# Two transformer blocks on one core: waits moved at the first key unit, at the hand-overs between stages, in the recurrence and at the end

## The reference

```python
# block 1
hx = modulate(rms_norm(x, g_pre_mix), sh_m, sc_m)      # sh_m, sc_m ... from silu(c) @ w_mod + b_mod
hc = modulate(rms_norm(ctx, g_pre_mix), csh_m, csc_m)
...                                                     # attention and retention of hx @ w_in, hc @ w_in
x_new = x + gt_m * rms_norm(mix_x, g_post_mix)
x_new = x_new + gt_f * rms_norm(swiglu(hf, w_ffn_in, w_ffn_out), g_post_ffn)
# block 2
x = x + 0.5 * swiglu_2(rms_norm_2(x, ffn1_norm), ffn1_gate, ffn1_up, ffn1_down)
z = rms_norm_2(x, mix_norm) @ w_in                      # zq, zf, zi, zg, zb, zc, zu
o_h = hgrn2_chunkwise(q, 1 - f, zi, log(f))             # the recurrence, f from zf and lb_param
y_conv = zb * causal_depthwise_conv(zc * zu, conv_w)
x = x + concat(y_hgrn, y_conv) @ w_out
km, vm = split(rms_norm_2(mem, mem_norm) @ w_kv_mem)    # memory attention
x = x + att @ w_o_mem
x = x + 0.5 * swiglu_2(rms_norm_2(x, ffn2_norm), ffn2_gate, ffn2_up, ffn2_down)
return rms_norm_2(x, final_norm)
```

## Time and profile before

| | |
|---|---|
| median of 3 runs | 1061.64 us (1059.79 to 1061.7) |
| the profiled execution's own time | 1061.17 us |
| its span in the trace | 1059.4 us |
| TensorE busy | 1020.1 us, 96% of the span |
| VectorE busy | 596.0 us, 56% |
| ScalarE busy | 494.4 us, 47% |
| mean DMA rate over the span | 178 GB/s |
| weight units transferred | 156 of 1024 KB |

### The profile page before, as it was taken

One profiled execution on the slowest core, in us unless ns is written; L12 is line 12 of the kernel. 1 busy time (PEld: TensorE's weight loads), 2 busy tenths in 40 slices (PEclk: granted clock), 3 DMA queues, 4 the chain that ended last, 5 costly groups with the idle time before them and its releaser, 6 DMA issues.

```text
span 1059.4 us, 13255 instructions
## 1 busy us (share of the span) xinstructions
PE 1020.1 (96%) x5148; PEld 834.7 (79%) x5148; DVE 596.0 (56%) x689; ACT 494.4 (47%) x598; POOL 0.2 (0%) x4
## 2 busy tenths in 40 slices
PE   4989999999999999999999999999999999999996
PEld 3867876897788888888888887788878778888885
DVE  4186386766755554475555545857666456555543
ACT  6253446646543444364444433674346445444431
POOL 0000000000000000000000000000000000000000
PEclk8999999999999999999999999999999999999998
DMA  9928585003554555556555555443243236455541
GB/s 370 417 88 321 208 299 217 28 1 120 199 188 170 198 187 174 194 181 212 183 187 184 184 198 191 163 178 136 80 159 130 109 119 217 181 189 186 179 159 40
DMA packets 26542, 188.71 MB, mean 178 GB/s; under 512 B 2944, under 2 KB 3200, under 8 KB 3968
## 3 DMA queue, kind: packets, MB, share of 16 engines
q1 hardware_dynamic: 25920, 185.63, 48.2%
q10 hardware_dynamic: 576, 2.43, 0.6%
HBM read 187.00 MB, written 1.05 MB: 178 GB/s over the span
## 4 chain that ended last, share of the span: by engine, by line
PE 90%; DVE 5%; ACT 2%; issue 1%; DMA 1%; SPq 0%; DVEq 0%; ACTq 0%
PE bank L1739 25%; PE bank L1741 25%; PE bank L1740 25%; PE bank L1814 2%; DVE w_lo L1129 2%; PE bank L2118 1%; PE bank L1795 1%; PE bank L2011 1%; PE bank L2000 1%; DMA raw<-in_weights 1%; PE bank L2211 1%; ACT w_hi L626 1%; PE bank L2322 1%; PE bank L2048 1%; PE bank L2027 1%
## 5 line engine op out<-in xcount | busy, mean ns | idle before, releaser
L1129 DVE TENSOR_TENSOR w_lo<-raw,w_hi 128x2048 fp32r<-128x2048 f32 (+1 forms) x149 | 338.6, 2276 | 272.5 <-ACT w_hi L626 272.4
L626 ACT ACTIVATE w_hi<-raw 128x2048 fp32r<-128x2048 f32 x148 | 283.1, 1916 | 261.2 <-PE bank L1741 249.4
L1739 PE MATMUL bank<-w_hi,hT_hi 128*128 128x512 f32 (+1 forms) x848 | 335.2, 395 | 7.5 <-issue 5.0
L1741 PE MATMUL bank<-w_hi,hT_lo 128*128 128x512 f32 (+1 forms) x848 | 329.7, 389 | 0.0
L1740 PE MATMUL bank<-w_lo,hT_hi 128*128 128x512 f32 (+1 forms) x848 | 329.3, 388 | 0.0
L1739 PEld LDWEIGHTS bank<-w_hi,hT_hi 128*128 128x128 f32 x848 | 159.7, 188 | 47.2 <-issue 10.9
L1741 PEld LDWEIGHTS bank<-w_hi,hT_lo 128*128 128x128 f32 x848 | 159.6, 188 | 33.6
L1740 PEld LDWEIGHTS bank<-w_lo,hT_hi 128*128 128x128 f32 x848 | 159.8, 188 | 31.3 <-issue 0.2
L1739 PE MATMUL bank<-w_hi,gT_hi 128*128 128x512 f32 x264 | 103.3, 391 | 0.0
L1741 PE MATMUL bank<-w_hi,gT_lo 128*128 128x512 f32 x264 | 102.8, 389 | 0.0
L1740 PE MATMUL bank<-w_lo,gT_hi 128*128 128x512 f32 x264 | 102.7, 389 | 0.0
(11 more groups left out here) (286 smaller groups left out, 993.2 us busy)
## 6 DMA issues: line engine op xcount, KB each, us to landing
raw<-in_weights SPq DMA_DIRECT2D x156, 1024.0 KB, 4.8
arena<-in_first_mods SPq DMA_DIRECT2D x8, 1024.0 KB, 18.0
memV<-in_own_mods SPq DMA_DIRECT2D x8, 1024.0 KB, 4.8
arena<-in_const ACTq DMA_DIRECT2D x1, 1088.0 KB, 5.0
memV<-in_mem SPq DMA_DIRECT2D x1, 1024.0 KB, 6.8
x_res<-in_x SPq DMA_DIRECT2D x1, 1024.0 KB, 18.0
arena<-in_ctx SPq DMA_DIRECT2D x1, 1024.0 KB, 13.8
out<-xn SPq DMA_DIRECT2D x2, 512.0 KB, 2.7
```

The source lines that it names most:

```text
L626: act.activation(w_hi[:, v_slot, :], raw[:, u_slot, :], ACT.Copy).then_inc(hi_ready, 1)
L1129: ins = dve.tensor_tensor(w_lo[:, v_slot, n], raw[:, u_slot, n], w_hi[:, v_slot, n].bitcast(F32), ALU.subtract)
L1739: pe.matmul(out, hi, rhi, start=start, stop=False)
L1741: return pe.matmul(out, lo, rhi, start=False, stop=stop)
```

## The change

**The first key unit.** TensorE transposes the memory first and then does modulation unit 0, where it did that unit first. The first key unit goes through a new function, `first_keys`: 16 matmuls of high x high that wait only for ScalarE's parts, 16 of low input x high weight, 16 of high input x low weight. ScalarE and VectorE take two quarters of `memT` ahead of the first weight split and two behind it; ScalarE loads the table of the square root ahead of the memory's arrival. The second keys follow modulation unit 1, and units 2 and 3, 4 and 5, 6 and 7 are done in pairs. Both engines split `W_IN` ahead of the modulation's columns, and six key products stand behind `mod_T(0)` instead of two. The banks of the keys change:

```diff
-    for u, b in enumerate([0, 1, 3, 0]):
+    for u, b in enumerate([5, 1, 0, 3]):
         plan.streamed(("memK", u), b)
...
```

On ScalarE:

```diff
+            load_table(ACT.Sqrt)
             norm_stats(mem_in, lambda e: e.wait_ge(sem("mem_loaded"), 16))
             norm_scale(mem_in, mem_in)
+            split_T("memT", col("mem_norm"), hi=memT_hi, qs=[0, 1])
             split_to(W_K + 1)
-            split_T("memT", col("mem_norm"), hi=memT_hi)
+            split_T("memT", col("mem_norm"), hi=memT_hi, qs=[2, 3])
...
+            split_to(W_IN + 1)
             mod_row_out(0)
-            split_to(W_IN + 1)
+            split_to(W_IN + 2)
+            split_T(None, shifted=True, hi=hT_hi, qs=[0, 1])
             keys_out(3)
-            split_T(None, shifted=True, hi=hT_hi, qs=[0, 1])
-            split_to(W_IN + 2)
```

On VectorE (the last pieces: `W_IN` split ahead of `mod_columns`, and unit `W_UP[0]` of the first feed-forward split behind its input's parts instead of ahead of them):

```diff
+            split_T("memT", col("mem_norm"), hi=memT_hi, lo=memT_lo, qs=[0, 1])
             low_to(W_K + 1)
-            split_T("memT", col("mem_norm"), hi=memT_hi, lo=memT_lo)
+            split_T("memT", col("mem_norm"), hi=memT_hi, lo=memT_lo, qs=[2, 3])
...
-            low_to(W_K + 4)
+            low_to(W_IN + 1)
             mod_columns(0)
...
-                if n < 3:
+                if 0 < n < 3:
                     low_to(W_IN + n + 1)
...
-            low_to(W_UP[0] + 1)
             split_T("ffn0T", shift=(a_ffn, mod[:, 24:32, 0]))
             low_to(W_UP[0] + 3)
```

```diff
+            def low_last(stage, v, half, outs, first, last, after_high=None, after_input_low=None):
+
+                pe.wait_ge(hi_ready, v + 1)
+                s = v % RING
+                quarters = (2 * half, 2 * half + 1)
+                weights = lambda w, q, e: w[:, s, (2 * (q % 2) + e) * 512:(2 * (q % 2) + e) * 512 + 512]
+                for q in quarters:
+                    pe.wait_ge(sem("T_hi"), T_HI[stage, q])
+                    for e in range(2):
+                        for tb, out in enumerate(outs):
+                            pe.matmul(out[:, :], hT_hi[:, 2 * q + e, tb * P:(tb + 1) * P], weights(w_hi, q, e),
+                                      start=(first and q == quarters[0] and e == 0), stop=False)
+                if after_high:
+                    after_high()
+                for q in quarters:
+                    read_out(pe, (stage, q))
...
+                if after_input_low:
+                    after_input_low()
+                pe.wait_ge(split_ready, v + 1)
...
-            mod_unit(0)
             pe.wait_ge(sem("fixed_loaded"), 16)
             transpose_input("memT", mem_in)
+            mod_unit(0)
+            first_keys()
             mod_unit(1)
-            for q in range(4):
-                read_out(pe, ("memT", q))
-            take(key_products(0), 16)
-            mod_unit(2)
             take(key_products(1), 16)
+            for m in range(2, 4):
+                mod_unit(m)
...
             keys = key_products(3)
             take(keys, 8)
-            mod_unit(6)
-            take(keys, 4)
-            mod_unit(7)
+            for m in range(6, 8):
+                mod_unit(m)
             take(keys, 2)
             mod_T(0)
-            take(keys, 2)
+            take(keys, 6)
...
-                        order.sort(key=lambda o: o[2])
+                        order.sort(key=lambda o: (o[0], o[2]) if f == 2 else o[2])
...
-            transpose_x("ffn2T", added(("mem_out",)))
-            ffn(2, "ffn2T")
+            transpose_x("ffn2T", added(("mem_out",)), [0])
+            ffn(2, "ffn2T", lambda: transpose_x("ffn2T", added(("mem_out",)), [1]))
```

**Ahead of the second mixture.** ScalarE issues two of its three small transfers a stage earlier and the third behind its copies of the input instead of ahead of them:

```diff
-            used(W_DN[1] + UP - 1)
-            for dst, src, name in [(const2, io["const2"], "const2_loaded"),
+            for dst, src, name in [(rows[:, 0, :], io["final_norm"].to_broadcast([P, D]), "final_loaded"),
                                    (lb_p.rearrange("p a n -> p (a n)"), io["lb_param"].to_broadcast([P, D]), "lb_loaded"),
                                    (head_row, io["hgrn_out_norm"].to_broadcast([P, 512]), "head_row_loaded")]:
                 act.dma_start(dst, src).then_inc(sem(name), 16)
-            pre_norm("mix2T", x_added(("down", 1), 0), col("mix_norm"), W_IN2)
+            ffn(1)
+            split_to(W_IN2 + 2)
+
+            split_T("mix2T", col("mix_norm"))
+            used(W_DN[1] + UP - 1)
+            act.dma_start(const2, io["const2"]).then_inc(sem("const2_loaded"), 16)
+            norm_stats(x, x_added(("down", 1), 0))
+            split_to(W_IN2 + 3)
```

The lower bounds of the recurrence's gate (`lb`), with a reciprocal of 512 columns, move on VectorE from behind `pre_norm("mix2T")` into `ffn(1)`, one group behind each of three weight splits; the exponential on ScalarE moves with them:

```diff
+                if f == 1:
+                    dve.wait_ge(sem("lb_loaded"), 16)
+                    chain(dve.tensor_tensor(lb, lb_p[:, 0, :], lb_p[:, 1, :], ALU.max))
+                    dve.tensor_tensor(lb_p[:], lb_p[:], over_heads(lb, 2, 512), ALU.subtract).then_inc(sem("lb_diff"), 1)
+                    low_to(dn + 5)
+                    dve.wait_ge(sem("lb_exp"), 1)
+                    chain(dve.tensor_tensor(lb, lb_p[:, 0, :], lb_p[:, 1, :], ALU.add))
+                    low_to(dn + 6)
+                    chain(dve.reciprocal(lb, lb))
+                    low_to(dn + 7)
...
```

**The recurrence.** The transposes `uT` move into the unit of step 5 (banks 0 and 1), the transposes `bT` ahead of the pair scores of step 6. On ScalarE the copies of `uT` move ahead of `zb`, and the copy `crossT` and the load of the Silu table move behind the two copies of the convolution. On VectorE:

```diff
-            for level in range(LEVELS + 1):
+            for level in range(LEVELS):
...
-                if level == LEVELS:
-                    convolution()
+                if level == LEVELS - 1:
+                    decayed(LEVELS)
                 if level:
                     keep_pairs(level - 1, ("pairs", level - 1))
-                if level == LEVELS:
-                    gated_convolution()
-                else:
-                    low_to(W_IN2 + 9 + level)
+                low_to(W_IN2 + 9 + level)
+                if level == LEVELS - 2:
+                    convolution()
...
+            gated_convolution()
+            keep_pairs(LEVELS - 1, ("pairs", LEVELS - 1))
```

**The end.** The last weight unit of `ffn(2)` is ordered by token block. VectorE and ScalarE then add, square and scale by token block and column half; the second token block's first half is scaled on ScalarE, and `out` leaves in three transfers (512, 256 and 256 KB) instead of two of 512 KB:

```diff
+            dve.wait_ge(sem("last_products"), 1)
+            last_add(0, 0)
+            last_add(0, 1)
+            last_mean(0)
+            dve.wait_ge(sem("last_products"), 2)
+            last_add(1, 0)
+            last_rstd(0)
+            last_out(0, 0)
+            dve.wait_ge(split_used, W_DN[2] + UP)
+            last_add(1, 1)
+            last_mean(1)
+            read_out(dve, ("down", 2, 1, 0))
+            dve.tensor_tensor(xn[:, 1, 0:512], x[:, 1, 0:512], rows[:, 0, 0:512], ALU.mult).then_inc(sem("last_gained"), 1)
+            last_out(0, 1)
+            last_rstd(1)
+            last_out(1, 1)
```

199 lines of the change are left out of this document (134 added, 65 removed).

## The result

The changed kernel took 1049.32 us (median of 4 runs, 1048.3 to 1049.62) against 1061.67 for the kernel before (4 runs, 1059.79 to 1061.72): a ratio of 0.9892, 95% interval 0.9878 to 0.9906. The forecast was 1048.3. The profiled execution took 1049.6 us with a span of 1047.8, which is 11.6 less than before.

The account below looks back on a forecast made before the run. TensorE, busy 96% of the span, was taken as the bound, leaving 39.3 us of idle time and low-clock stretches. Terms summed to 13.1 us off 1061.17, giving 1048.1, taken as 1048.3; range 1042 to 1054.

Parts of the forecast that it names:

- Start: From the kernel's beginning to `W_IN`: key waits, low clock and a context wait go, 8.2 us faster, bounds 6 to 9.
- Chain (c): Start: `W_IN` lands at 43.4 and is split by 47.5, so its first product comes at 49.95, 7.4 us earlier.
- (a): Start: TensorE's own work, which would reach the end of the six key products at 49.
- First feed-forward: First feed-forward: the stall moves to a 1.7 us wait for `w_lo`, 0.4 us slower; bounds -1.7 and +2.7.
- rival (2): Both feed-forwards: the clock falls at the new waits, each fall costing 2.3 us, total 1053 to 1054; chance 0.14.
- Second mixture: Second mixture: earlier hand-over gives -2.3 us, lower bounds moved out -0.9; 3.2 us faster, bounds -2 and -3.8.
- The cover in `ffn(1)`: In `ffn(1)`: 6.8 us free on VectorE hide the moved lower bounds' longest piece, 3.35; failure would cost 1 to 3.
- Memory attention and last feed-forward: Their hand-overs: later half 1 transposes delay low parts and weight splits by 1.65 us, costing +0.5 and +1.6.
- (1): Three hand-overs: `w_lo` is never late and the old waits go too, 21.2 us faster, 1040; chance 0.10.
- (3): Start: transfers bound it, with `W_IN` 5 us later; the gain there would be 3, total 1053.5; chance 0.06.
- (4): Start: slower, the clock stays at 1.2 GHz through the keys, some 22 us more, total 1069; chance 0.03.
- (5): Whole kernel: nothing gained, since the waits are filled by others of the same size all along; chance 0.02.

Follow-up runs that it names:

- e8: Changed kernel, but the first key unit goes through the old function, which waits for all low parts: 1053.29 us.
- e9: Changed kernel, but `W_IN` is split behind the modulation's row and columns again, as before: 1052.28 us.
- e2: Changed kernel, but at `mix2T`, `xattT` and `ffn2T` VectorE splits the second unit between the low parts of quarters 1 and 2: 1044.24 us.
- e4: Changed kernel, but at `xattT` and `ffn2T` all transposes stand ahead of the first unit, as before the change: 1045.81 us.
- e11: Changed kernel with the end as before (last unit's order, adds, norm of whole rows, two scalings, two transfers): 1051.65 us.
- e5: Changed kernel, but the square root's table is loaded ahead of the last feed-forward's norm, with the scratch buffer `warm` left as it was: 1047.77 us.
- e7: Changed kernel with the start (key units, modulation, `W_IN`'s split, table load, banks) put back as before on all three engines: 1057.58 us.
- e10: Changed kernel, but the lower bounds are computed in the second mixture again, behind its norm, instead of in `ffn(1)`: 1053.15 us.
- e3: Changed kernel, but the square root's table is loaded ahead of the last feed-forward's norm, with scratch buffer `warm` one float wider: 1053.09 us.

## Why the prediction was right, and which steps were off

The forecast was 1 us below the measured median, and its sum was off by 1.5 (13.1 for 11.6). By its own words the sum gives 1048.1 + 0.5 = 1048.6 for the median; the 1048.3 has no working. All seven terms have the right sign. The total is closer than its parts, by luck: the start gained 0.9 more than forecast, and the rest 2.4 less. No run takes out the recurrence's edits or the new hand-over at `mix2T`, so these two rest on the distances alone. By its steps:

**Start, -8.2, measured -9.1.** `W_IN` came at 49.95, the very number of the forecast, but for another reason. Chain (c), `W_IN` landing and being split, was said to end last, 1 us behind (a). In the trace the split ends at 47.2 (44.88 and 2.29) and the row waits 0.32 more, until 47.50, for TensorE's own `mod_T`: (a) ended last. e8 shows it (4.6 us on TensorE go straight through) and e9 too (the row stays where it is without the split). The two sums happened to agree, which was luck. The missing 0.8 lay behind `W_IN`: the kernel before has two waits at the context, 0.80 at 64.06 and 0.17 at 65.33, and 1.6 us went with them. The forecast counted the first alone, and at its bracket; a wait costs more than that (last section).

**First feed-forward, +0.4, measured +1.9: the term that was mis-sized.** The stall came where forecast, for `w_lo`, 1.97 for 1.7. Most of the rest was the clock, rival (2), which I had at 0.14. The distance from this wait to the mixture's first product is 382.1 us in the changed kernel (265.34 to 647.45), e2, e4, e9 and e11, and 380.9 to 381.0 in e5, e7, e8 and e10, with the same code in between. Those of 382.1 have a granted clock of 0.5 to 0.6 behind the wait and the others 1.00, all with the same bracket of 1.97 or 1.98. So the fall costs 1.2 us, not the 2.3 that I gave it, and comes in some executions and not in others. A clock of 0.57 over 4 us takes 1.7; some of that is given back, because the slower TensorE comes too late for the next wait. That wait is in every trace without the fall, as in e5, and in none with it:

```profile
267.39 0.47 PE L1804 MATMUL bank<-w_hi,hT_hi 128*128 128x512 f32 x1 [0.18 <-DVE w_lo L1160]
```

Without the fall the term is +0.7: waits of 1.97 and 0.18 for one of 1.72, and 0.25 for the second one's start (last section).

**Second mixture, -3.2, measured -2.7.** Both parts are there: 1.6 us are gained up to the third unit (2.3 forecast; the second unit started 2.3 earlier where 3.0 was said, and the third lost 0.6 of that), and 1.1 at the sixth (0.9 forecast). What failed is that I priced them as if they stood apart. e10 shows that without moving the lower bounds the hand-over's 1.6 is lost to VectorE's list, and 1.1 more than that, so the group's move was worth 3.8 beside the new hand-over and not 0.9. The cover in `ffn(1)`, which I priced at 1 to 3 us if it failed, held.

**Recurrence, -2.4, measured -2.5**, with the 1.09 gone and a wait of 1.01 left where 0.9 was said.

**Memory attention and last feed-forward, +0.5 and +1.6, measured +1.0 and +1.9.** The chain was right: the high parts, then the low parts of quarters 2 and 3 late (1.9 by the trace, 1.65 forecast), then everything behind them. e4 takes it out (3.75 back) and e2 fills it. The size was short because TensorE was at the second unit 0.5 earlier than reckoned and `w_lo` 0.3 later, so that it waited 0.8 there at both stages where "gained 0.1" stood. The table load's 1.28 was confirmed by e5; the drain that the Trainium skill (ScalarE: Activation LUTs, What ACT_TABLE_LOAD costs) adds behind it, by which this term would have been +3.0 (an estimate), did not show: in the changed kernel the load at 860.18 takes 1.28 and the next activation stands at 861.48, and e5 gained 1.29.

**End, -1.8, measured -1.9** (e11 gives it back), with 7.5 us behind the last matmul where 7.2 was said.

**The rivals.** (1), that the new waits don't come, is out: they all came. (2) came at one of its two places, in 6 of 11 traces, and at half its price. Its list of earlier waits, with one fall in four, left out the 3.93 of the start, behind which the clock was low too. (3), the transfers, is out: ScalarE splits `W_IN` from 42.94, so it had landed by then, and 43.4 was forecast. (4) is out by the granted clock of 1.00 behind the first keys, and (5) by the time. The range of the main case, 1044.5 to 1051.5, holds the result.

## What to carry to other kernels

Where one engine waits for another that works through a fixed list, find the idle time inside that list before moving anything on the waiting engine: here 1.9 us of VectorE at each of three hand-overs, filled by one split each, were worth 5 us, while letting TensorE start earlier there had only turned its own time into waits. Terms that draw on the same list are not added: price the second edit with the first one in place, as e10's two waits of 1.6 against the one of 0.89 show. And when an experiment adds even one float of scratch, take it from a buffer that is there, or its result may be that of the placement, as in e3.
